# Two score units of the prompt attention moved in front of a sample pair's last weighted sum, in a hybrid decoder layer

## What is computed

```python
sc = jnp.einsum('bqkgd,bckd->bqkgc', qg, kv_c[:, :, 0]).astype(jnp.float32) * scale   # "c": block means
pc = masked_softmax(sc, mc)
o_c = jnp.einsum('bqkgc,bckd->bqkgd', pc.astype(q.dtype), kv_c[:, :, 1])
...
ss = jnp.einsum('bqkgd,bqknsd->bqkgns', qg, g[..., 0, :]).astype(jnp.float32) * scale  # "s": selected blocks
o_s = jnp.einsum('bqkgns,bqknsd->bqkgd', ps.astype(q.dtype), g[..., 1, :])
...
sw = jnp.einsum('bqkgd,blkd->bqkgl', qg, kv_w[:, :, 0]).astype(jnp.float32) * scale    # "w": window
o_w = jnp.einsum('bqkgl,blkd->bqkgd', pw.astype(q.dtype), kv_w[:, :, 1])
...
o = jnp.sum(gates * o_br, axis=2).reshape(B, T, ATT_WIDTH)
y_att = rms_norm(o * jax.nn.silu(z_a), att_norm_g)
mix = jnp.concatenate([y_ssd, y_att], axis=-1) @ w_out
return x + gate[:, None] * mix
```

## Time and profile before

| | us |
|---|---|
| median of 3 runs | 866.78 |
| lowest, highest | 865.96, 870.12 |
| the profiled execution | 873.36 |
| its span, first to last instruction | 871.5 |
| TensorE busy in the span | 825.4 (95%) |
| VectorE, ScalarE, GpSimd busy | 524.8, 359.0, 263.4 |
| mean granted TensorE clock | 0.984 of full speed |

### The profile page before, as it was taken

One profiled execution on the slowest core, in us unless ns is written; L12 is line 12 of the kernel. 1 busy time (PEld: TensorE's weight loads), 2 busy tenths in 40 slices (PEclk: granted clock), 3 DMA queues, 4 the chain that ended last, 5 costly groups with the idle time before them and its releaser, 6 DMA issues. The chain is left out here.

```text
span 871.5 us, 20078 instructions
## 1 busy us (share of the span) xinstructions
PE 825.4 (95%) x8505; PEld 539.8 (62%) x8505; DVE 524.8 (60%) x1095; ACT 359.0 (41%) x739; POOL 263.4 (30%) x232
## 2 busy tenths in 40 slices
PE   3999999999999999999999999798999999999997
PEld 2447998877788766567555555555456565655563
DVE  2146553376789744556544536867878778776632
ACT  4041002011212255446334236854766656465623
POOL 2047888370000043235310110429401230301121
PEclk9899999999999999999999999989999999999999
DMA  9963165553220000300943550920102001112102
GB/s 300 336 208 106 49 191 207 237 193 114 80 75 1 24 6 1 95 3 1 354 148 119 175 175 7 262 72 8 44 15 87 2 28 50 28 51 74 62 3 97
DMA packets 45410, 89.04 MB, mean 102 GB/s; under 512 B 4388, under 2 KB 26076, under 8 KB 43210
## 3 DMA queue, kind: packets, MB, share of 16 engines
q1 hardware_dynamic: 38202, 54.94, 19.9%
q0 software_dynamic: 6080, 31.79, 10.5%
q10 hardware_dynamic: 1040, 1.05, 0.4%
HBM read 75.49 MB, written 16.40 MB: 105 GB/s over the span
## 5 line engine op out<-in xcount | busy, mean ns | idle before, releaser
L2204 PE MATMUL PS<-W,hT 128*128 128x512 f32 x256 | 113.0, 594 | 0.3 <-DVE W L1823 0.3
L1988 DVE CUSTOM_DVE_ANT_0 PS<-PS,consts 128x640 f32<-128x640 f32 (+5 forms) x96 | 77.4, 835 | 30.9 <-PE PS L2623 30.6
L2204 PEld LDWEIGHTS PS<-W,hT 128*128 128x128 f32 x256 | 47.9, 190 | 56.0 <-issue 54.8
L1105 POOL TENSOR_TENSOR Q<-Q,U 128x512 f32<-128x512 f32 x16 | 20.5, 1280 | 163.8 <-DVE U L2025 139.4
L1435 ACT ACTIVATE hT<-PS,small 128x128 f32<-128x128 f32 (+7 forms) x64 | 47.0, 740 | 49.0 <-DVE small L1988 47.7
L2590 PE MATMUL PS<-U,Y 128*128 128x512 f32 x128 | 60.2, 603 | 0.0
L2590 PE MATMUL PS<-U,Q 128*128 128x512 f32 x128 | 59.1, 598 | 0.0
L1435 ACT ACTIVATE T<-PS,small 128x640 f32<-128x640 f32 (+4 forms) x64 | 41.8, 667 | 22.7 <-DVE small L1988 21.6
L2004 DVE STREAM_TRANSPOSE hT<-hT 128x1024 f32<-128x1024 f32 (+6 forms) x29 | 42.8, 1488 | 1.3 <-ACT hT L1435 1.3
L2590 PEld LDWEIGHTS PS<-U,Q 128*128 128x128 f32 x128 | 23.5, 190 | 29.0 <-issue 28.9
L2623 PE MATMUL PS<-KTsw,W 64*128 64x512 f32 (+3 forms) x128 | 39.4, 517 | 0.3 <-ACT KcTs L1427 0.2
(11 more groups left out here) (545 smaller groups left out, 1845.5 us busy)
## 6 DMA issues: line engine op xcount, KB each, us to landing
W<-in_w_in SPq DMA_DIRECT2D x4, 2048.0 KB, 8.0
W<-in_w_ada SPq DMA_DIRECT2D x7, 1024.0 KB, 16.3
U<-in_x_prompt SPq DMA_DIRECT2D x8, 512.0 KB, 11.5
W<-in_w_ada SPq DMA_DIRECT2D x2, 2048.0 KB
U<-in_state_win_kv POOLq DMA_DIRECT2D x8, 512.0 KB
W<-in_x_prompt SPq DMA_DIRECT2D x8, 512.0 KB, 3.4
out_y_prompt<-W SPq DMA_DIRECT2D x8, 512.0 KB, 2.6
out_new_win_sample<-in_state_win_kv POOLq DMA_DIRECT2D x1, 4032.0 KB, 24.5
```

The lines of the kernel that those rows point to most:

```text
L1105: nc.gpsimd.tensor_tensor(Q3[:, i, :], Q3[:, i, :], spare, ALU.add).then_inc(s_added, 1)
L1988: ins = nc.vector.tensor_tensor_reduce(x, x, strip(u), 1.0, -NEG, ALU.add, ALU.min, sneg_m[u % 2][:, m:m + 1])
L2204: ins = nc.tensor.matmul(bank(z_bank(u)), hT3[:, k, i * P:(i + 1) * P], w, start=(k == 0), stop=(k == KT8 - 1))
```

## The change

Units 0 and 1 are no longer scored in the step list but inside the sample stage, in front of the last pair's page sum; the code of a score unit becomes a function. VectorE's combination of the last pair's rows moves from the sample stage to the place of SOFTMAX of unit 2. ScalarE waits for the samples' sum at unit 2 instead of at the start. The maxima's registers (`sneg_m`) move ten columns on, since the sample stage's sums are still alive. The whole order string is another one, with the same letters in the same numbers.

```diff
-        sneg_m = [st[:, 100 + 8 * n:108 + 8 * n] for n in range(2)]
+        sneg_m = [st[:, 110 + 8 * n:118 + 8 * n] for n in range(2)]
...
+        EARLY_SCORES = 2
...
-            "qqxsxyxssmwsvctxszqtxyksxtvscsxtkgxsmxcwvvasyxkwusmtgtxtspxoapptoorropoooxpctossxtvvkuptsxpcsvvvxsqx"
+            "qsxxyqxsscwmsztxvsqxktysvsxtcsxtmgwksxvxvcaysswxtutgksootooxoxopmoatrospsprcvxpvtxktusxstvvvpscxqotx"
...
-            act.wait_ge(s_smp_sum, 4)
             for (what, u), again in zip(STEPS, AGAIN):
...
+                        if u == EARLY_SCORES:
+                            act.wait_ge(s_smp_sum, 4)
                         for m in range(nh):
...
+            def sample_rows(p):
+                dve.wait_ge(s_smp_sum, p + 1)
+                if p:
+                    dve.wait_ge(s_ostored, 16 * p)
+                for n in range(4):
+                    q, k = slice(32 * n, 32 * n + 32), n % 2
+                    ins = nc.vector.tensor_tensor(orow[q], bank(6, 0, 384)[q].rearrange("p (n k d) -> p n k d", n=NBR, k=KVH)[:, :, k, :],
+                                                  ssum[q].unsqueeze(2).broadcast_to([32, NBR, HD]), ALU.mult)
+                ins.then_inc(s_orow, 1)
...
-                dve.wait_ge(s_smp_sum, p + 1)
-                if p:
-                    dve.wait_ge(s_ostored, 16 * p)
...
-                ins.then_inc(s_orow, 1)
-                dve.wait_ge(s_orow, p + 1)
+                if p < NB // 2 - 1:
+                    sample_rows(p)
+                    dve.wait_ge(s_orow, p + 1)
...
+                if (what, u) == ("SOFTMAX", EARLY_SCORES):
+                    sample_rows(NB // 2 - 1)
...
+            def score_unit(u):
...
                 pe.wait_ge(s_turned_act, 5 * p + 5)
                 pe.wait_ge(s_turned_dve, 5 * p + 5)
+                if p == NB // 2 - 1:
+                    for u in range(EARLY_SCORES):
+                        score_unit(u)
                 weighted_sum(bank(6, P, 2 * P), 0, pgs, NPG, 13, Vs3).then_inc(s_smp_sum, 1)
...
                 elif what == "S":
...
+                    if u >= EARLY_SCORES:
+                        score_unit(u)
```

More of the change, by code:

```diff
@@ L2470, in queries_turned @@
                 ins.then_inc(s_fill, 1)
+            def score_unit(u):
+                i, k, h, nh = UNITS[u]
+                a, n, step = keys(u)
+                if k == "c":
+                    pe.wait_ge(*EMPTY["QT", i, 0])
+                if u >= 2:
+                    pe.wait_ge(s_exp, u - 1)
+                if nh == 1:
+                    pe.wait_ge(s_swapped, 6)
+                base = u % 2 * 1024
+                if k == "c":
+                    for g in range(GQ):
+                        for kv, q in enumerate(HALF):
+                            at = base + kv * 512 + g * NCB
+                            ins = nc.tensor.matmul(PS[:, at:at + NCB], QD[i % 2][q, kv * GQ + g, :], KcT[q, 0:NCB], start=True, stop=True)
+                    ins.then_inc(s_scores, 1)
+                    return
+                if nh > 2:
+                    for x in range(2):
+                        o = PS[:, base + x * 512:base + x * 512 + nh // 2 * step].rearrange("p (h s) -> p h s", s=step)
+                        nc.tensor.matmul(o, identb, masks[:, 3 * P - step:].unsqueeze(1).broadcast_to([P, nh // 2, step]), start=True, stop=False)
+                for x, pair in enumerate(zip(*score_parts(u))):
+                    for half, (hh, lo, m, c) in enumerate(pair):
+                        stop = nh <= 2 or x == nh // 2 - 1
+                        ins = nc.tensor.matmul(PS[:, base + c:base + c + m], QD[i % 2][HALF[half], hh, :], keys_on(half, k, i, hh // GQ, lo, m),
+                                               start=nh <= 2, stop=stop)
+                ins.then_inc(s_scores, 1)
             for p in range(NB // 2):
@@ L2599, in _ @@
                 elif what == "S":
[L2600 to L2603, removed]
-                    if u >= 2:
-                        pe.wait_ge(s_exp, u - 1)
-                    if nh == 1:
-                        pe.wait_ge(s_swapped, 6)
-                    base = u % 2 * 1024
-                    if k == "c":
-                        for g in range(GQ):
-                            for kv, q in enumerate(HALF):
-                                at = base + kv * 512 + g * NCB
-                                ins = nc.tensor.matmul(PS[:, at:at + NCB], QD[i % 2][q, kv * GQ + g, :], KcT[q, 0:NCB], start=True, stop=True)
-                        ins.then_inc(s_scores, 1)
-                        continue
-                    if nh > 2:
-                        for x in range(2):
-                            o = PS[:, base + x * 512:base + x * 512 + nh // 2 * step].rearrange("p (h s) -> p h s", s=step)
-                            nc.tensor.matmul(o, identb, masks[:, 3 * P - step:].unsqueeze(1).broadcast_to([P, nh // 2, step]), start=True, stop=False)
-                    for x, pair in enumerate(zip(*score_parts(u))):
-                        for half, (hh, lo, m, c) in enumerate(pair):
-                            stop = nh <= 2 or x == nh // 2 - 1
-                            ins = nc.tensor.matmul(PS[:, base + c:base + c + m], QD[i % 2][HALF[half], hh, :], keys_on(half, k, i, hh // GQ, lo, m),
-                                                   start=nh <= 2, stop=stop)
-                    ins.then_inc(s_scores, 1)
+                    if u >= EARLY_SCORES:
+                        score_unit(u)
                 elif what == "CV":
```

14 lines of the change are left out of this document (5 added, 9 removed).

## The result

The changed kernel took 876.88 us (median of four executions, 873.39 to 881.79) where the kernel before took 867.55 beside it: a ratio of 1.0089, 95% interval 1.005 to 1.0128. With twelve executions each it came to 1.0054 [1.0033, 1.0074] and 1.0053 [1.0024, 1.0083]. So it is slower by about 0.5%, or 4 to 5 us, where 3 us less had been forecast.

A forecast was written before the change was run, and what follows sets the result against it. TensorE was taken as the bound, busy 825.4 of 871.5 us, leaving idle and half-clock time to gain. Lead 2.2 plus clock 0.8 gave -3.0, nothing behind 578: 866.8 to 863.8 us, range 859.5 to 868.5.

The forecast's parts named there:

- The walk of the opening: From the seam to the third PV: step times in the new order, ending with that PV 2.2 us earlier, at 563.0.
- The hole I take as coming again: TensorE's unexplained 1.85 us idle stretch before the first output projection: assumed to recur, so no gain was counted.
- the -2.2: Lead at the third PV, 2.2 us earlier than 565.27, said to remain at the first output projection (578.15).
- The -0.8 for the clock: Half-clock stretch from 564: shorter pauses were to save a third of its estimated 2.8 us loss, 0.8 us.
- so does all behind them: Samples' rows land 2.8 us later, and everything behind them too: the store and GpSimd's products and addition.
- The port: SBUF port pair shared by GpSimd and VectorE: GpSimd's 2.80 us product could hold VectorE's small product at the first BACK.
- Rival 1: Opening before 578: shorter pauses remove both half-clock stretches, gaining 6.5 us to 860.3, or 858.5 with the hole; chance 0.32.
- a lead at 578 goes to the end: Behind the first output projection TensorE is full, so time gained by 578 was to reach the kernel's end.
- Rival 4: Behind 578 the new order brings a wait tuned away before: 2 to 5 us slower than forecast, to 868; chance 0.07.
- the prediction's sign for this rival: Behind 610 us: TensorE idle by more than 5.4 us would show that the new order is worse there.
- Rival 3: First BACK: a slip of 0.9 us makes VectorE wait for GpSimd's product, second PV 2.3 later, 871.3; chance 0.06.
- the 3.0 of one execution: Whole kernel: total gain of 3.0 us counted on the profiled 873.36, then subtracted from the median of 866.8.

The follow-up runs named there:

- after: The changed kernel as first measured and profiled, against the kernel before: median 876.88 us, ratio 1.0089; the profiled execution took 873.39 us.
- before: The kernel without the change, as first profiled: that execution took 873.36 us; its median beside the changed kernel was 867.55 us.
- order_only: The kernel before with the changed kernel's whole order string but the old seam: ratio 1.0035 to the kernel before.
- late_weights_before: The kernel before with the 3 MB of output weights held back until the third exponential: ratio 1.0009 to the unmodified kernel before.
- after_again: The changed kernel, unmodified, measured again with more executions: ratio 1.0054 to the kernel before.
- after_third: The changed kernel, unmodified, measured once more beside others on the same chip: ratio 1.0053 to the kernel before, median 874.74 us.
- late_rows: The changed kernel with residual rows, gates and norm weights (2 MB) issued only when CV of tile 2 is done: ratio 1.0013 to the kernel before.
- more_load_after: The changed kernel with 2 MB of additional DRAM-to-DRAM copies queued behind the norm weights: ratio 1.0053 to the kernel before.
- before_again: The kernel before, unchanged, measured again: ratio 1.0005.

## Why the prediction was wrong

**The walk of the opening held.** Forecast and found in after: VectorE at unit 0 538.2, 538.46; ScalarE's first exponential 539.5, 539.83; unit 2's 546.1, 546.47; second PV 554.7, 554.61; GpSimd's long product 553.3, 552.85; third PV 563.0, 563.65, so 1.6 earlier than before and not 2.2; the samples' GATE asked for at 560.5, 560.94. No wait for the samples' sum remained on VectorE, and the half-clock stretch at 564 did not come: the PV took 2.08.

**The step that failed** is "The hole I take as coming again: no row says what it hangs on", with 1.85, and with it the -2.2 that was to remain behind the hole. I treated as a duration what is a date. The hole is the time from TensorE's arrival to that of its packet. Whoever arrives earlier waits longer, and the packet came no more than 0.75 us earlier. The 3.4 us of lead at 568.05 became 2.6 more of hole (4.47 for 1.85). The -0.8 for the clock failed too: the pause was followed by half clock, which made CV 0.84 longer and the output projection 1.2. Two rows did bear on it: the DMA share of 0.93 in the earlier trace rows, just ahead of the hole, and the instruction queues that the page lists. And "so does all behind them", of the samples' rows that come 2.8 us later, was followed for GpSimd alone; the loads that SyncE issues behind GpSimd's products came 2.3 us later as well.

**What of the loss is shown, and what is not.** That moving the rows removes the slowdown is shown, three times, against the changed kernel on the same chip; in these traces the hole is 0 to 0.44 us and the half clock behind it is gone. How much of the 4 to 5 us of the medians (873.73 over 869.48, and 874.74 over 869.60) is the hole and how much other effects of the same load (the samples' rows, the values for the next tiles) was not separated. From the start of the seam to the end of the span, three traces of before take 336.3, 335.6 and 333.0 us, and three of the changed kernel 336.1, 336.9 and 336.6: 1.6 more in the mean, where 3.0 less was forecast, so 4.6 are to be explained. The hole is 2.1 in the mean of the one and 3.9 of the other: 1.8. Half clock between 530 and 590 costs 4.6 and 5.7, by the granted clock of each microsecond: 1.1, where 0.8 less was counted on. Added up that is 3.7 of the 4.6, an account and not an experiment. The port adds 0.1 by the means of its product. Against a full account by the hole stand order_only, slower with a hole of 0.97, and the load added to the old kernel, which did not clearly slow it. The medians' difference is larger than the traces', and that remainder has only the scatter of three traces to explain it.

**Rival 1**, the opening closes, came true only where the rows were moved: 37.5 to 38.1 us instead of 42.9 in five traces. But the median ratios were 0.9986 to 1.0013, not the 0.9925 of its price. Three of these traces (early rows, twice, and with the port's wait) take 331.7, 332.4 and 330.6 us from the seam to the end, 3.4 less than before in the mean, and the medians show 0 to 1.2. So the prediction's "a lead at 578 goes to the end" is not borne out by the medians either. The three traces of before may be long ones: late_weights_before, whose ratio is 1.0009, takes 331.1. **Rival 4** is not borne out as its cause. TensorE's waits for ScalarE and VectorE behind the output projection are 5.3 to 6.2 us with the new string and 2.9 to 5.1 in the old kernel, but 4.6 to 5.9 with the new seam and the old string as well, and the idle time marked "issue" shrank meanwhile, from a range of 3.9 to 5.2 to one of 2.3 to 4.0. In the stretch that the prediction named, behind 610, TensorE is idle 6.0 us for 5.4: the prediction's sign for this rival came, by 0.6 us. With the rows early the new string costs nothing against the old one (0.9986 and 0.9994); with the rows late and the old seam it cost 1.0035, which stays open. Why the shorter opening does not reach the medians is open: it would take many more executions of each kernel to see 2 us.

**Rival 3** had 0.06, and its distance was put at 0.9 us; GpSimd's product started 0.33 us behind VectorE's in after, and 2.31, 2.02, 1.42 and 0.26 ahead of it in after_again, after_third, late_rows and more_load_after, with 0.52, 0.81, 1.40 and 2.57 us for VectorE's product: it waits for what is left of the 2.80. So it came in most of these traces, at another price each time, and the old kernel pays as much in the mean. A rival with a threshold near the scatter of its inputs is not a case with a chance but a cost with a share.

**The median.** I carried the 3.0 of one execution over to the median. The profiled execution of before was slow for its kernel and had its PV at half clock (as its two later traces do), which is just the case in which the hole is short; the range was built around that one draw, and left 0.09 for slower.

## What to carry to other kernels

An idle stretch marked "issue", in the middle of equal products, is a date and not a duration: find the packet of the queue marked "instruction" in the DMA view, and see which loads are in flight when it is due. Before speeding up the engine ahead of such a place, move the large loads away from it, or the gain is eaten there and, if the clock falls behind the pause, more than eaten. Where two engines race for a port within less than the start times scatter, look at several traces, not at one.

## What the runs showed of the hardware

- By packet count and size TensorE's instructions travel in packets of 16 KB, 256 instructions, on the same DMA engines as the data (the page lists both queues as shares of the 16). TensorE went on 2.4 to 3.0 us after the packet, with full and with idle engines. With the 2 MB of rows in flight the packet came 4.6 to 6.1 us behind the start of the block before it, and 0.8 to 2.3 with the rows moved.
- The products of PV use up 256 instructions in about 2.1 us (128 records and their weight loads, 2.08). In every trace a run of them meets a hole of 1.5 to 2.1 us at one boundary, between 590 and 606 us, in after at a DMA share of 0.01.
- Stretches at half clock (granted clock 0.50) came at other places in each execution of the same kernel: in before from 564 and from 574, in before_again from 553 and from 570. Between 530 and 590 they cost 3.4 to 5.1 us in three traces of before and 1.7 to 3.4 in four traces of the changed kernel with the rows moved. The scatter of 2 to 3 us between executions may be partly theirs; that was not tested.
- VectorE's small product with both inputs in SBUF waited out GpSimd's 2.80 us product: 2.57 when it came 0.26 behind its start, and 0.17 when it came 0.33 ahead. This agrees with what the prediction took from the Trainium skill, in "SBUF — State Buffer", section "SBUF: two separate sides".
